# A 31-tap convolution moved from vector taps to block-diagonal matmuls, in a two-layer hybrid decoder step

## The reference, cut to what matters

```python
h = x + 0.5 * rms_norm(swiglu(rms_norm(x, f1_pre), f1_wg, f1_wu, f1_wd), f1_post)
p_all = rms_norm(h, m_pre) @ w_in            # A | B | C | D side by side
ya = conformer_conv(A); yb = gla_mixer(B); yc = short_conv(C); yd = forgetting attention(D)
h = h + rms_norm(concatenate([ya, yb, yc, yd]) @ w_out, m_post)
h = h + 0.5 * rms_norm(swiglu(...), f2_post)

def conformer_conv(pa, buf, conv_w, conv_b, ln_g, ln_b):
    val, gate = jnp.split(pa, 2, axis=-1)
    a = val * jax.nn.sigmoid(gate)
    xpad = jnp.concatenate([buf, a], axis=1)             # 30 rows of history ahead
    y = causal_depthwise(xpad, conv_w) + conv_b           # 31 taps, each of 256 channels by itself
    return jax.nn.silu(layer_norm(y, ln_g, ln_b)), xpad[:, -30:]
```

## Time and profile before

| | us |
|---|---|
| median of 3 runs | 1197.14 |
| lowest, highest | 1190.25, 1197.24 |
| the profiled execution, its own time | 1192.01 |
| its span | 1190.2 |

### The profile page before, as it was taken

The page is one execution under the profiler, slowest core; times in us unless marked ns, Lnnn a source line. Parts: engine busy times, 40 slices in busy tenths (PEclk is TensorE's granted clock), DMA queues, the critical chain, the costliest instruction groups (busy, mean ns, idle before and its releaser), DMA issues.

```text
span 1190.2 us, 25496 instructions
## 1 busy us (share of the span) xinstructions
PE 1125.6 (95%) x8736; PEld 1080.3 (91%) x8736; DVE 778.5 (65%) x994; ACT 563.9 (47%) x900; POOL 381.9 (32%) x451
## 2 busy tenths in 40 slices
PE   6999999877999999999989999998889999999996
PEld 6999999767989899999989999987678999999995
DVE  5666543999775766654566665358997657666546
ACT  5544544641246654454454445445312655544544
POOL 3222211455933322221132222124667233222112
PEclk9999999998799999999999999999978899999998
DMA  7655566322334465555435555744222254555552
GB/s 255 212 180 183 177 209 214 123 89 82 105 101 146 138 196 183 188 167 191 158 128 181 188 177 180 222 154 143 89 91 88 90 181 143 196 183 181 167 192 73
DMA packets 64744, 188.69 MB, mean 159 GB/s; under 512 B 9594, under 2 KB 20866, under 8 KB 64514
## 3 DMA queue, kind: packets, MB, share of 16 engines
q1 hardware_dynamic: 64642, 187.38, 48.1%
HBM read 183.97 MB, written 3.38 MB: 157 GB/s over the span
## 4 chain that ended last, share of the span: by engine, by line
PE 81%; DVE 10%; issue 7%; ACT 2%; DMA 0%; DVEq 0%; SPq 0%; POOL 0%; ACTq 0%; POOLq 0%
PE ub L287 24%; PE ub L288 23%; PE ub L289 23%; DVE resid L945 2%; DVE z_t L942 2%; DVE w_lo L274 1%; PE mb L592 1%; PE ub L307 1%; PE mb L625 1%; PE ub L308 1%; PE ub L309 1%; DVE proj L1184 1%; ACT w_hi L268 1%; DVE lv L1002 1%; DVE hg_lo L931 1%
## 5 line engine op out<-in xcount | busy, mean ns | idle before, releaser
L274 DVE TENSOR_TENSOR w_lo<-raw,w_hi 128x1024 fp32r<-128x1024 f32 x339 | 456.8, 1352 | 362.7 <-ACT w_hi L268 362.1
L287 PE MATMUL ub<-hg_hi,w_hi 128*128 128x264 f32 x1648 | 484.5, 294 | 25.1 <-DVE proj L1184 22.3
L268 ACT ACTIVATE w_hi<-raw 128x1024 fp32r<-128x1024 f32 x339 | 346.4, 1028 | 299.2 <-PE ub L289 264.8
L288 PE MATMUL ub<-hg_lo,w_hi 128*128 128x264 f32 x1648 | 477.8, 290 | 0.0
L289 PE MATMUL ub<-hg_hi,w_lo 128*128 128x264 f32 x1648 | 477.1, 290 | 0.0
L287 PEld LDWEIGHTS ub<-hg_hi,w_hi 128*128 128x128 f32 x1648 | 321.9, 195 | 34.2 <-DVE w_lo L274 29.9
L288 PEld LDWEIGHTS ub<-hg_lo,w_hi 128*128 128x128 f32 x1648 | 322.2, 196 | 0.4
L289 PEld LDWEIGHTS ub<-hg_hi,w_lo 128*128 128x128 f32 x1648 | 320.1, 194 | 0.0
L287 PE MATMUL ub<-act_hi,w_hi 128*128 128x264 f32 x704 | 200.5, 285 | 0.0
L289 PE MATMUL ub<-act_hi,w_lo 128*128 128x264 f32 x704 | 199.6, 284 | 0.0
L288 PE MATMUL ub<-act_lo,w_hi 128*128 128x264 f32 x704 | 199.1, 283 | 0.0
(11 more groups left out here) (231 smaller groups left out, 1264.7 us busy)
## 6 DMA issues: line engine op xcount, KB each, us to landing
raw<-in_w_gu SPq DMA_DIRECT2D x179, 512.0 KB, 3.7
raw<-in_w_dn SPq DMA_DIRECT2D x64, 512.0 KB, 3.6
raw<-in_w_in SPq DMA_DIRECT2D x44, 512.0 KB, 3.5
raw<-in_w_dn SPq DMA_DIRECT2D x32, 384.0 KB, 3.5
raw<-in_w_out SPq DMA_DIRECT2D x16, 512.0 KB, 3.4
pages<-in_cache_k SPq DMA_DIRECT2D x32, 128.0 KB, 2.3
pages<-in_cache_v SPq DMA_DIRECT2D x32, 128.0 KB, 2.8
con<-in_con SPq DMA_DIRECT2D x1, 1444.0 KB
```

Source lines behind the costliest of these rows:

```text
L268: eng.activation(w_hi[:, slot, 0:w], raw[:, slot, 0:w], ACT.Copy).then_inc(*sig("hi_ready", reps))
L274: eng.tensor_tensor(w_lo[:, slot, 0:w], raw[:, slot, 0:w], w_hi[:, slot, 0:w].bitcast(F32), ALU.subtract)\
L287: eng.matmul(out, a_hi, x_hi[:, k0 + k, :], start=(first and k == 0), stop=False)
L288: eng.matmul(out, a_hi, x_lo[:, k0 + k, :], start=False, stop=False)
```

## The change

The convolution of the prompt leaves DVE and POOL. On the host the taps are laid out as `acm`: with a tap index t = 4j + s (s the shift, j the step, a 32nd tap of zero), row 32s + m and column (c, j, q) hold the tap t of channel 32q + m of tile c. POOL builds from it in step 0 the stationary operands `cw`, 64 blocks of 128x32, each four diagonal blocks of 32x32 under one another. SP copies `a_pad` in 16 transfers within SBUF into `xs`: partitions 32s to 32s + 31 hold channels 32q to 32q + 31, shifted by s columns, for each q. `xs` lies in slots 14 and up of `proj`, which later units overwrite. PE then makes 64 matmuls in step 12, 8 steps j by 4 channel groups q by 2 tiles c; each contracts all 128 rows (four taps of 32 channels), has 32 columns of weights, and writes 32 partitions of PSUM. ACT copies the sums out with the bias in step 13. The layer norm moves from steps 20 to 24 to steps 16 to 19 (its Silu to 22). The gate units get slots 4 and 5 and the value units 8 and 9, so that ACT's sigmoids move from step 10 to step 8, with their two loads of function tables. In "out", the tiles of A come second, not last. The sums of the 8 decode columns move from DVE's step 18 to 14.

```diff
-ALR, FG, BQ, BK, AV, AG, BG, BV, DQ, ... = 0, 1, 2, 3, 4, 6, 8, 10, 12, ...
+ALR, FG, BQ, BK, AG, BG, AV, BV, DQ, ... = 0, 1, 2, 3, 4, 6, 8, 10, 12, ...
-YB, YC, YD, YA = 0, 2, 4, 6
+YB, YA, YC, YD = 0, 2, 4, 6
+SHIFTS, STEPS = 4, 8
+XS = TP + SHIFTS * (STEPS - 1)
+        cw = sb("cw", [P, 2, STEPS, 4, 32])
+        xs = proj[:, DKK:24, :].rearrange("p a b -> p (a b)")[:, 0:8 * XS].rearrange("p (c q t) -> p c q t", c=2, q=4)
...
@@ SP, mix
+                if n == 10:
+                    sp.wait_ge(*at(l, "a_in", 1))
+                    for s in range(SHIFTS):
+                        for q in range(4):
+                            sp.dma_start(xs[32 * s:32 * s + 32, :, q, :], a_pad[32 * q:32 * q + 32, :, s:s + XS]).then_inc(*sig("xs_in", n=16))
@@ PE
+            def conv_taps(l):
+                after(l, xs_in=16 * 4 * SHIFTS, a_cw=1, b_sp=1, b_la=1)
+                for c in range(2):
+                    for j in range(STEPS):
+                        for q in range(4):
+                            mm = pe.matmul(mb[2][32 * q:32 * q + 32, c * TP:(c + 1) * TP], cw[:, c, j, q, :],
+                                           xs[:, c, q, SHIFTS * j:SHIFTS * j + TP], start=j == 0, stop=j == STEPS - 1)
+                    mm.then_inc(*sig("a_conv"))
+                if n == 12:
+                    conv_taps(l)
                 if n == 16:
+                    conv_sum(l)
                     gla_outputs(l)
...
+                    conv_var(l)
@@ ACT, mix
-                if n == 10:
+                if n == 8:
                     act.preload_act_table(ACT.Sigmoid)
-                    after(l, proj=10)
+                    after(l, proj=8)
+                if n == 13:
+                    after(l, a_conv=2)
+                    for c in range(2):
+                        act.activation(ymix[:, YA + c, 0:TP], mb[2][:, c * TP:(c + 1) * TP], ACT.Identity, bias=...).then_inc(*sig("a_all"))
@@ DVE, mix
-                if n in TAPS:
-                    conv_taps(l, *TAPS[n])
@@ POOL, mix, n == 0
+                    pool.tensor_tensor(cw[:, :, :, :, :].rearrange("p c j q m -> p (c j q) m"),
+                                       const("eye", 32).unsqueeze(1).to_broadcast([P, 64, 32]),
+                                       par[:, PAR["acm"]:PAR["acm"] + 64].unsqueeze(2).to_broadcast([P, 64, 32]), ALU.mult).then_inc(*sig("a_cw"))
@@ POOL, mix
-                if n in (13, 15, 17):
...
```

More of the change, by code:

```diff
@@ L881, in mix @@
                                        bias=par[:, PAR["alb"] + c:PAR["alb"] + c + 1]).then_inc(*sig("a_y"))
+                    for h in range(H):
+                        probabilities(l, h)
+                if n == 23:
+                    round_mixed(l, YA)
+                    after(l, d_o=1)
+                    act.activation(ymix[:, YD:YD + 2, 0:TP], mb[2][:, :].rearrange("p (a b) -> p a b", a=2), ACT.Copy).then_inc(*sig("d_y"))
             def round_mixed(l, first):
@@ L905, in outp @@
                     output_tile(l, 1, n, ub[n % 4], n % 2, reps)
-                for first in range(2, KD, 2):
+                for first in (YC, YD):
                     round_mixed(l, first)
@@ L1013, in level_mask @@
                     dve.tensor_tensor(scores[:, :], scores[:, :], level[:, :], ALU.add).then_inc(*sig("b_asc"))
[L1015 to L1024, removed]
             def mix(l, n):
@@ L1050, in mix @@
                     level_mask(l, n - 7)
-                if n == 12:
-                    after(l, a_in=2)
+                if n == 14:
+                    after(l, a_dp=2)
+                    dve.tensor_reduce(ymix[:, YA:YA + 2, TP:NT], a_prod[:, :, :, :], AX.X, ALU.add).then_inc(*sig("a_dr"))
+                    after(l, a_dr=1)
+                    dve.tensor_tensor(ymix[:, YA:YA + 2, TP:NT], ymix[:, YA:YA + 2, TP:NT],
+                                      par[:, PAR["acb"]:PAR["acb"] + 2].unsqueeze(2).to_broadcast([P, 2, TD]), ALU.add).then_inc(*sig("a_db"))
                 if n == 15:
@@ L1079, in mix @@
                     dve.tensor_scalar(tail[:, :], tail[:, :], -1.0, dstat[:, 0:1], ALU.mult, ALU.add).then_inc(*sig("d_ct"))
[L1080 to L1086, removed]
+                if n == 17:
+                    after(l, a_sum=1, a_all=2, a_db=1)
+                    for c in range(2):
+                        dve.scalar_tensor_tensor(ymix[:, YA + c, :], ub[2][:, 0:NT], -1.0 / 256, ymix[:, YA + c, :], ALU.mult, ALU.add)\
+                           .then_inc(*sig("a_cen"))
                 if n in (19, 20):
@@ L1291, in mix @@
                 if n == 10:
-                    after(l, a_sg=1, past=PAST)
-                    pool.tensor_tensor(a_pad[:, :, TAPS_A - 1:], proj[:, AV:AV + 2, 0:TP], proj[:, AG:AG + 2, 0:TP], ALU.mult).then_inc(*sig("a_in"))
+                    after(l, a_sg=1, past=PAST, proj=10)
+                    pool.tensor_tensor(a_pad[:, :, TAPS_A - 1:TAPS_A - 1 + TP], proj[:, AV:AV + 2, 0:TP], proj[:, AG:AG + 2, 0:TP], ALU.mult).then_inc(*sig("a_in"))
                     pool.tensor_tensor(a_dec[:, :, :, TAPS_A - 1], proj[:, AV:AV + 2, TP:NT], proj[:, AG:AG + 2, TP:NT], ALU.mult)\
                         .then_inc(*sig("a_in"))
+                if n == 13:
+                    after(l, a_in=2)
+                    for c in range(2):
+                        pool.tensor_tensor(a_prod[:, c, :, :], a_dec[:, c, :, :],
+                                           par[:, PAR["acw"] + c * TAPS_A:PAR["acw"] + (c + 1) * TAPS_A].unsqueeze(1).to_broadcast([P, TD, TAPS_A]),
+                                           ALU.mult).then_inc(*sig("a_dp"))
                 if n == 12:
```

106 lines of the change are left out of this document (38 added, 68 removed).

## The result

| | before | after |
|---|---|---|
| median, us | 1197.19 (4 runs) | 1230.22 (4 runs) |
| lowest, highest | 1190.25, 1197.52 | 1226.07, 1233.29 |
| the profiled execution | 1192.01 | 1233.29 |
| its span | 1190.2 | 1231.2 |

The changed kernel takes 1.0287 times as long, 95% interval 1.0242 to 1.0332: slower, by 33 us between the medians. The forecast was 1233. The profiled execution of after is the longest of its four, and that of before lies 5.2 us under its median, so the spans differ by more than the medians, by 41.0.

The account below looks back on a forecast made before the run. DVE was taken to bound each mixer up to `decode_scores`, PE after it. Per layer 17.2 + 2.4 - 1.0 + 7.2 - 7.1 = +18.7 us, 37.4 for both, giving 1233 us; range 1215 to 1262.

Parts of the forecast that it names:

- The sum: All terms of the mixer added up: +18.7 us a layer, 37.4 us for both layers.
- first parts: Each mixer's stretch up to PE's first `decode_scores`, taken as bound by DVE, 66 us from unit 3 on.
- second part: Each mixer from `decode_scores` on, 290.5 to 386.6 us in layer 0, bound by PE; forecast again 96 us at 0.88.
- `cw` on POOL: Building `cw` at the mixer's start takes 4.8 us and holds up DVE's splits, +4.5 us.
- an issue of a copy, and 16: SP's sixteen copy issues in step 10: 0.5 us each, 8.0 in all, with bounds 6.1 and 10.4.
- unit 12 late: PE starts unit 12 at 285.3 instead of 268.14 us, 17.2 late, 4.5 of it from `cw`.
- unit 12 at half clock: After PE stands some 14 us, unit 12 takes 5.6 us instead of 3.1, +2.4.
- idle ahead of 13, 14: PE no longer waits for DVE's copies ahead of these units; the 1.0 us ahead of unit 13 goes, -1.0.
- 64 matmuls: The convolution on PE: 128 records at 0.056 us, +7.2 us a layer, with 6.5 to 14 in the range.
- unit 13 to `decode_scores`: PE's stretch from unit 13's start, without taps ahead of DVE's copies: 10.1 us instead of 17.2, -7.1.
- the hold on SP: In step 10 unit 14's load queues behind the `a_in` wait and 16 issues; its split ends at 284.9, not 267.7.
- first rival: Unit 14's load is hidden, so SP's wait costs the weights nothing: +8.2 us a layer, 1213; 6 in 100.

## Why the prediction was right

The time, 1230 for 1233, came out by its own steps; here each is set against layer 0. The sum, 37.4 for two layers, is met best by the first parts of the profiled executions, 18.6 and 18.7 longer. The spans differ by 41.0, of which 3.4 lie in the second part, and the medians by 33.0. So the sum came out for the first part, and that the time itself came within 3 us is in part luck.

| step | forecast, us | measured, us |
|---|---|---|
| `cw` on POOL | 4.8 | 3.65 |
| delay of DVE by it | +4.5 | +3.4 (`a_pad` at 268.24 for 264.85) |
| an issue of a copy, and 16 | 0.5, 8.0 | 0.65, 10.37 |
| unit 12 late | 17.2 | 18.7 |
| unit 12 at half clock | 5.6 | 4.95, at a mean of 0.58 |
| idle ahead of 13, 14 | 0, 0 | 0, 0 |
| 64 matmuls | 7.2 | 7.1 |
| unit 13 to `decode_scores` | 10.1 | 9.4 |
| `decode_scores` late | 18.7 | 18.8 |
| second part | 96.1 at 0.88 | 97.6 at 0.86 |

**What held.** The step that decides, the hold on SP, was right in its place and its chain, and was shown in both directions by taking it out (21 us) and putting it alone into the old kernel (28 us). Of the first rival, the hidden load, the run with the loads first is the test: 1209, 4 below its 1213. Its copies had landed at 281.18 for the rival's 281.4, but its matmuls then took 9.58 us and not 7.2, the first half of them at a granted clock of 0.50.

**What was mis-sized.** Errors of both signs met. The issues took 0.65 each, the upper of the two bounds. The earlier trace rows had six in a row at just that; the forecast chose a value nearer to the first gap, of 0.48, although the copies do stand in a row. That made 2.4 too little. `cw` made 1.1 too much: its price was scaled in proportion from `q_lv`, 2.42 for 1024 elements, and twice the elements took 1.5 times as long. What is left of the two, 1.3 too little, was taken back by unit 12, which ran only in part at half clock, and by the stretch behind unit 13, each some 0.7. The first split of the mixer, named as a sign at about 6 us, took 4.53.

**The matmuls.** 0.056 a record, what was taken. The Trainium skill (TensorE: Matmul & The Clock Gate, "Measured speedup vs the span model") gives 2.38x for three column tiles, and the estimate of 9.1 us that the prediction worked out from it is too high here: 128 records in 7.11 us, or 0.056 against the 0.226 of unpacked ones, is four times for four tiles, both at a granted clock of 1.00. The measurement decides.

**The second part.** Forecast as unchanged; it took 1.5 us more a layer, 3 in all, at a lower clock, and the prediction had named another length as a sign of being wrong. The table above answers it: the same instructions took 91.5 to 97.9 us at 0.93 to 0.86, in kernels of either kind and in both layers of one execution. The changed kernel's relative with its copies behind the loads has 96.2 at 0.88, as before. So the 1.5 is not shown to come from the change, and what sets the clock in that part stays open. By the granted clock, the profiled execution of after was at the slow end of this.

**What the prediction did not see** is that this loss wasn't the change's nature but its placing. Its first rival gave the matmuls themselves +8.2 a layer; with both queues and the build out of the way the first part is 0.4 and 0.2 us longer than before: they cost nothing, net of the taps that they replace. The forecast of that rival left out that the convolution's own wait for its copies could go as well.

## What to carry to other kernels

A wait on a queue that also issues loads costs what stands behind it: list the next load and when it is due, then put the wait behind it; here one digit was worth 21 us. Then look for who waits for the copies. Many small copies have a price in issues, not in bytes; count them, and share them between two queues, or put them where nothing behind them is due. When a rearranged kernel wins, run the rearrangement without the new algorithm: here the times couldn't tell the two apart. And before a stretch's clock is laid to a change, compare the same stretch in both layers of one execution.

## What the runs showed of the hardware

- A copy of 71 KB within SBUF lands in 2.1 us, but sixteen in a row are issued 0.65 us apart on SP and eight at 0.66 on ACT (5.27): issuing sixteen takes five times as long as one takes to land.
- DVE's splits and POOL's instructions, each with both operands in SBUF, didn't run beside one another. The split that began at 224.29, 0.2 us after `cw`, ended at 228.82, 1.1 after `cw`'s end at 227.74; the one at 229.09 ended at 231.71, again 1.1 after the zeroing of `qm`, which itself took 2.92, for 1.94 in the earlier trace rows, since its first us lay beside the end of the split before. DVE's copy out of PSUM at 228.74, beside that same zeroing, took its usual 0.41. The Trainium skill (SBUF — State Buffer, "SBUF: two separate sides") calls the shared pair "an **exclusive lock**, not a bandwidth split"; the trace agrees.
- Four groups of 32 columns pack fully in float32 (7.11 and 14.02 us for 128 and 256 records), although all four write one PSUM tile, `mb6`.
